# A two-layer hybrid block with 64 routed experts: the order of the expert weight loads, the expert slots, and three reorderings on the engines

## What is computed

```python
def moe_ffn(h, router_w, router_bias, w_gate, w_up, w_down, sh_gate, sh_up, sh_down):
    scores = jax.nn.sigmoid((h @ router_w).astype(jnp.float32))
    ...                                  # 4 of 8 groups, then the 8 best of their experts
    w = jnp.take_along_axis(scores, idx, axis=1)
    w = w / jnp.sum(w, axis=-1, keepdims=True) * ROUTED_SCALE
    shared = (jax.nn.silu(h @ sh_gate) * (h @ sh_up)) @ sh_down
    return routed_experts(h, idx, w, w_gate, w_up, w_down) + shared
...
    # of one expert e and its tokens xb
    hid = jax.nn.silu(xb @ w_gate[e]) * (xb @ w_up[e])      # 1024 -> 256
    return (hid @ w_down[e]) * wt[:, None]                  # 256 -> 1024
```

## Time and profile before

| | us |
|---|---|
| median of 3 runs | 2142.07 (2141.47 to 2149.24) |
| the profiled execution's own time | 2148.33 |
| its span, first to last instruction | 2146.50 |
| TensorE matmul busy | 1657.4 (77%) |
| VectorE, ScalarE, GpSimd busy | 905.9, 569.5, 347.5 |
| mean granted clock of TensorE | 0.91 |
| HBM read | 557.87 MB |

### The profile page before, as it was taken

One profiled execution on the slowest core, in us unless ns is written; L12 is line 12 of the kernel. 1 busy time (PEld: TensorE's weight loads), 2 busy tenths in 40 slices (PEclk: granted clock), 3 DMA queues, 4 the chain that ended last, 5 costly groups with the idle time before them and its releaser, 6 DMA issues. The chain is left out here.

```text
span 2146.5 us, 39607 instructions
## 1 busy us (share of the span) xinstructions
PE 1657.4 (77%) x11491; PEld 714.8 (33%) x11492; DVE 905.9 (42%) x3060; ACT 569.5 (27%) x1173; POOL 347.5 (16%) x357
## 2 busy tenths in 40 slices
PE   3999799858878888888886499698556656766675
PEld 2545554422223223322322455454212211212221
DVE  2245563364444444444446336543522322322334
ACT  2142352212322333333231214242111211221221
POOL 0001300002222222222220001210011111111110
PEclk8999799989999999999999699789888888988888
DMA  8315510447999899998837823813499989999974
GB/s 272 130 70 193 190 60 1 176 172 285 376 373 412 342 375 365 405 365 333 346 114 313 273 80 118 334 32 147 174 361 364 412 344 414 409 401 356 407 300 181
DMA packets 165603, 578.28 MB, mean 269 GB/s; under 512 B 24956, under 2 KB 29792, under 8 KB 148648
## 3 DMA queue, kind: packets, MB, share of 16 engines
q1 hardware_dynamic: 134592, 515.49, 61.9%
q0 software_dynamic: 24256, 60.03, 7.5%
q10 hardware_dynamic: 6696, 1.98, 0.4%
HBM read 557.87 MB, written 37.89 MB: 278 GB/s over the span
## 5 line engine op out<-in xcount | busy, mean ns | idle before, releaser
L1225 PE MATMUL bank<-arena 128*32 128x512 f32 x4160 | 544.1, 645 | 291.6 <-DMA arena<-in_exp_w_up 171.1
L1225 PEld LDWEIGHTS bank<-arena 128*32 128x32 f32 x4160 | 118.0, 115 | 494.8 <-issue 312.6
L692 POOL DMA_INDIRECT yrows<-arena x128 | 130.1, 1016 | 915.4 <-ACT arena L925 915.4
L1250 PE MATMUL bank<-arena 128*32 128x512 f32 x2048 | 247.0, 598 | 18.3 <-issue 16.5
L1735 DVE TENSOR_TENSOR arena<-arena,bank 64x512 f32<-64x512 f32 x130 | 88.4, 680 | 353.0 <-ACT arena L907 353.0
L920 ACT ACTIVATE arena<-bank 128x128 f32<-128x128 f32 x128 | 35.5, 278 | 685.6 <-PE bank L1281 685.6
L673 POOL DMA_INDIRECT arena<-hrows,arena x134 | 137.2, 1024 | 149.5 <-DVE arena L1709 108.5
L1693 DVE COPY arena<-arena 128x12 bf16 (+1 forms) x272 | 63.6, 234 | 193.4 <-issue 193.4
L991 PE MATMUL bank<-arena 128*128 128x512 f32 (+3 forms) x384 | 131.6, 504 | 11.7 <-DVE arena L1391 11.7
L1215 PEld LDWEIGHTS bank<-arena 128*128 128x128 f32 x528 | 73.8, 209 | 110.6 <-issue 110.6
L994 PE MATMUL bank<-arena 128*128 128x512 f32 (+1 forms) x256 | 100.0, 552 | 0.0
(11 more groups left out here) (304 smaller groups left out, 1910.2 us busy)
## 6 DMA issues: line engine op xcount, KB each, us to landing
arena<-in_exp_w_gate SPq DMA_DIRECT2D x128, 1024.0 KB
arena<-in_exp_w_up SPq DMA_DIRECT2D x128, 1024.0 KB
arena<-in_exp_w_down SPq DMA_DIRECT2D x128, 1024.0 KB
arena<-in_w_ada SPq DMA_DIRECT2D x10, 3072.0 KB
arena<-yrows SPq DMA_DIRECT2D x24, 1024.0 KB, 16.2
arena<-in_w_ada SPq DMA_DIRECT2D x8, 2048.0 KB
arena<-in_w_in SPq DMA_DIRECT2D x8, 2048.0 KB
arena<-in_w_out SPq DMA_DIRECT2D x4, 2048.0 KB
```

The lines of the kernel that those rows point to most:

```text
L692: pool.indirect_dma_start(out=yrows, out_offset=bass.IndirectOffsetOnAxis(ap=SIXS[u], axis=0), in_=YSB[u], in_offset=None, bounds_check=2 ...
L1225: ins = pe.matmul(bank[0][r:r + UNIT, :], XGT[:, c, un, hh, :], wv[un][:, :, hh, c, :], start=(c == 0), stop=(c == 3))
L1250: ins = pe.matmul(bank[2][r:r + UNIT, :], HIDT[:, c, UNIT * un:UNIT * un + UNIT], wv[un][:, c, cg * 512:(cg + 1) * 512], start=(c == 0), s ...
```

## The change

- **Order of the loads.** Refilling goes by expert n: first gate and up of expert n+4 (after the last gate-and-up product of expert n), then down of expert n+3 (after the last down product of expert n-1). So on the queue gate and up stand one expert ahead of down. Down of expert 3 is no longer loaded ahead of the loop, and down of the last expert is issued behind it. `TABP` gets a leading zero, so that expert n-1's entry exists for n = 0, and is read twice for each expert.
- **Semaphores.** Gate and up count on `sp_up`, not on `sp_land`, and SP no longer waits for a slot's last loads to have landed before it refills it.
- **Slots.** `exp_slot` gives expert 2's slot the place over `rH`, and expert 3's the third ring place; the first four experts are then loaded in the order 0, 1, 2, 3 (before: 0, 1, 3, 2), behind the same four events.
- **TensorE.** `meta` ("picking") moves from the head of an iteration to behind the down product of the one before; the table word is loaded once for each block, one block ahead, behind the transposes of the tokens, and carried in two registers; `b // 2` and `b % 2` are worked out behind the gate-and-up product.
- **ScalarE.** `silu` is cut in two, and the copy of the tokens (`xe`) stands between `lower_rows` and `silu`.

```diff
@@ -113,7 +113,8 @@
-        ring = [rRING + 6144 * k for k in range(3)] + [rH]
+        ring = [rRING + 6144 * k for k in range(3)]
+        exp_slot = [ring[0], ring[1], rH, ring[2]]
@@ -233,7 +234,7 @@
-        TABP = arena[0:1, o:o + NE].bitcast(I32); o += NE
+        TABP = arena[0:1, o:o + NE + 1].bitcast(I32); o += NE + 1
@@ -269,7 +270,8 @@
-        sp_land = [sem(f"sp_land{k}") for k in range(NSLOT)]
+        sp_land = [sem(f"sp_land{k}") for k in range(3)]
+        sp_up = [sem(f"sp_up{k}") for k in range(NSLOT)]
@@ -526,45 +526,50 @@
                 def load_up(e, k):
-                    w = at(ring[k], 2, 2, 4, HID)
+                    w = at(exp_slot[k], 2, 2, 4, HID)
                     for j, src in enumerate((eg, eu)):
...
                                      src[bass.ds(l * NE + e, 1)].rearrange("a (h p c) n -> p (a h) (c n)", h=2, c=4)
-                                     ).then_inc(sp_land[k], 16)
+                                     ).then_inc(sp_up[k], 16)
                 def load_down(e, k):
-                    sp.dma_start(at(ring[k] + 4096, 2 * DM),
+                    sp.dma_start(at(exp_slot[k] + 4096, 2 * DM),
                                  ed[bass.ds(l * NE + e, 1)].rearrange("a (p c) n -> p (a c n)", c=2)).then_inc(sp_dn[k], 16)
+                def blocks_up_to(j):
+                    return sp.snap((sp.value_load(TABP[0:1, bass.ds(j, 1)], min_val=0, max_val=MAXU) + 1) // 2)
+
...
-                    units_up_to = sp.value_load(TABP[0:1, bass.ds(i * NSLOT + u, 1)], min_val=0, max_val=MAXU)
-                    used = sp.snap((units_up_to + 1) // 2)
-                    sp.wait_ge(sp_land[u], i * 32 + (base_land[u] + 32))
-                    sp.wait_ge(sp_dn[u], i * 16 + 16)
-                    sp.sem_inc(sp_go, 1)
-                    sp.wait_ge(pe_gu, used + 1)
+                    k = (u + NSLOT - 1) % NSLOT
+                    sp.wait_ge(pe_gu, blocks_up_to(i * NSLOT + u + 1) + 1)
                     sp.sem_inc(sp_go, 1)
                     load_up(i * NSLOT + (NSLOT + u), u)
-                    sp.wait_ge(pe_dn, used + 1)
+                    sp.wait_ge(pe_dn, blocks_up_to(i * NSLOT + u) + 1)
                     sp.sem_inc(sp_go, 1)
-                    load_down(i * NSLOT + (NSLOT + u), u)
-
-
-                for e in (0, 1, 3, 2):
-                    if e < 3:
+                    load_down(i * NSLOT + (NSLOT + u - 1), k)
+
+
+                for e in range(NSLOT):
+                    if e < 2:
                         sp.wait_ge(*done_of[P_OUT + e])
-                    else:
+                    elif e == 2:
                         sp.wait_ge(pe_sh, 4)
                         sp.wait_ge(pool_hr, 16 * NTS)
+                    else:
+                        sp.wait_ge(*done_of[P_SH])
                     load_up(e, e)
-                    load_down(e, e)
+                    if e < NSLOT - 1:
+                        load_down(e, e)
                 sp.wait_ge(v_tab, 1)
...
                         reload(i, u)
+                sp.wait_ge(pe_dn, blocks_up_to(NE - NSLOT) + 1)
+                sp.sem_inc(sp_go, 1)
+                load_down(NE - 1, NSLOT - 1)
                 for k in range(NSLOT):
-                    sp.wait_ge(sp_land[k], base_land[k] + 32 * (NE // NSLOT))
+                    sp.wait_ge(sp_up[k], 32 * (NE // NSLOT))
                     sp.wait_ge(sp_dn[k], 16 * (NE // NSLOT))
@@ -900,26 +905,30 @@
-                def silu(val, free):
+                def lower_rows(val, free):
                     act.wait_ge(pe_gu, val + 1)
...
+
+                def silu(val):
                     act.wait_ge(v_gu, val)
...
                 xe(1)
-                silu(1, None)
+                lower_rows(1, None)
                 xe(2)
+                silu(1)
                 act.preload_act_table(ACT.Silu)
...
                         act.activation(HIDT, bank[5][:, 0:2 * SLOTS].rearrange("p (c s) -> p c s", c=2), ACT.Copy).then_inc(a_h, 1)
-                        silu(i * 2 + (u + 2), i * 2 + (u + 1))
+                        lower_rows(i * 2 + (u + 2), i * 2 + (u + 1))
                         xe(i * 2 + (u + 3))
+                        silu(i * 2 + (u + 2))
                         act.wait_ge(pe_dn, i * 2 + (u + 2))
@@ -1217,7 +1226,7 @@
-                    wv = [at(ring[k], 2, 2, 4, HID) for k in ks]
+                    wv = [at(exp_slot[k], 2, 2, 4, HID) for k in ks]
@@ -1230,9 +1239,9 @@
-                    pe.wait_ge(sp_land[k], e * 8 + (base_land[k] + 32 - 8 * k))
+                    pe.wait_ge(sp_up[k], e * 8 + (32 - 8 * k))
...
-                        pe.wait_ge(sp_land[k2], e * 8 + (base_land[k2] + 40 - 8 * k2))
+                        pe.wait_ge(sp_up[k2], e * 8 + (40 - 8 * k2))
@@ -1242,7 +1251,7 @@
-                    wv = [at(ring[k] + 4096, 2, DM) for k in ks]
+                    wv = [at(exp_slot[k] + 4096, 2, DM) for k in ks]
@@ -1251,9 +1260,12 @@
-                def experts_of(b):
...
-                    both = pe.value_load(TABK[0:1, bass.ds(b, 1)], min_val=0, max_val=2 * NE - 2)
+                def experts_word(b):
...
+                    return pe.value_load(TABK[0:1, bass.ds(b, 1)], min_val=0, max_val=2 * NE - 2)
...
+                def experts_of(both):
@@ -1287,7 +1299,11 @@
-                _, _, step = experts_of(0)
+                word = experts_word(0)
+                word_now = pe.alloc_register(f"word_now{l}")
+                word_next = pe.alloc_register(f"word_next{l}")
+                pe.reg_mov(word_now, word)
+                _, _, step = experts_of(word)
@@ -1299,12 +1315,12 @@
+                meta(4, 3)
+                pe.reg_mov(word_next, experts_word(1))
...
-                    meta(b + 4, b + 3)
-                    e, slot, step = experts_of(b + 1)
-                    half = pe.snap(b // 2)
-                    odd = pe.snap(b % 2)
+                    word = pe.snap(word_next)
+                    e, slot, step = experts_of(word)
@@ -1317,11 +1333,15 @@
                     in_slots(slot, step, up_and_turn)
+                    half = pe.snap(b // 2)
+                    odd = pe.snap(b % 2)
                     with pe.If(odd == 0):
...
                         turn_tokens(1, half * 16 + 32)
-                    now, slot_now, step_now = experts_of(b)
+                    now, slot_now, step_now = experts_of(pe.snap(word_now))
+                    pe.reg_mov(word_now, word)
+                    pe.reg_mov(word_next, experts_word(b + 2))
                     pe.wait_ge(a_h, b + 1)
@@ -1330,6 +1350,7 @@
+                    meta(b + 5, b + 4)
@@ -1610,7 +1631,8 @@
-                dve.wait_ge(v_pcl, 5)
+                dve.memset(TABP[0:1, 0:1], 0).then_inc(v_pcl, 1)
+                dve.wait_ge(v_pcl, 6)
@@ -1672,7 +1694,7 @@
-                link(dve.tensor_copy(TABP, PEND[0:1, :]))
+                link(dve.tensor_copy(TABP[0:1, 1:NE + 1], PEND[0:1, :]))
```

More of the change, by code:

```diff
@@ L426, in landed @@
             return sp_land[k], 16 * sum(d for m, d in enumerate(dmas_of[:n + 1]) if slot_of(m) == k)
-        base_land = [16 * sum(d for m, d in enumerate(dmas_of) if slot_of(m) == k) for k in range(NSLOT)]
         with nc.Block() as block:
```

## The result

The changed kernel took **2071.20 us** (median of four executions, 2068.59 to 2071.68), the kernel before beside it 2143.94 (2141.47 to 2149.24, four): a ratio of 0.9655, 95% interval 0.9634 to 0.9677. The profiled execution took 2068.59 us with a span of 2066.8, against 2148.33 and 2146.5: 79.7 us less. Later the same file ran twice more, in other sets of runs on two chips, and took 2095.63 and 2097.32 us, with the kernel before unchanged at 2147.

A forecast was written before the change was run, and what follows sets the result against it. TensorE, held by its sequencer, was taken to bound layer 0, and a loop of waits around loads layer 1. 42 + 32 + 2 = 76 us off gave 2066 us from the median, range 2036 to 2106.

The forecast's parts named there:

- rival 2: Layer 0: another wait takes the gap ahead of the gate-and-up product, layer 0 keeps 8 us; 2100 us, chance 0.13.
- Layer 1, forecast 32: Layer 1's loop: the new load order keeps the queue full and fills the holes, 32 us less, bounds 15 and 41.
- The loop of waits: Layer 1: SP's queue stands behind the down product, this behind the next gate-and-up product, that behind loads; no engine full.
- rival 1: Loads can't be packed closer, 414 GB/s not holding for 500 us; 2127 us, chance 0.05.
- Rival 3: Layer 1: the loop of waits stays, SP still behind a down product; layer 1 gives 10, 2088 us, chance 0.12.
- Layer 0, forecast 42: Layer 0's loop, paced by TensorE: 0.75 us less a block, capped by loads, 42 us less, bounds 25 and 58.
- rival 4: Gathers starve TensorE: a fuller queue makes GpSimd's gather later than its reader needs; slower, 2174 us, chance 0.04.
- the loads' limit of 49: Layer 0: what loads allow, 45 us of fillable DMA time plus 2.5 and 2; smaller than TensorE's 58.
- the gap shrinks to nothing: Layer 0, TensorE's wait ahead of the gate-and-up product, mean 0.86 us: it closes, taken as 0.75 us a block.
- the cover of SiLU and the product behind it: ScalarE's SiLU and product L1737 come up to 0.6 us later, covered by 24 matmuls (2.78 us) before the hidden transposes.
- It is what makes this gain possible: ScalarE's token copy ahead of SiLU comes 0.4 us or more earlier, so the wait for it doesn't hold the product.
- the 45 on the loads' side: Layer 0, 500 to 1075 us: DMA share 0.94 against 1.02 when full, so 45 us can be filled.

The follow-up runs named there:

- no_gather: The changed kernel with the loop's gathers replaced by a plain copy of 16 rows (products come out wrong): 78.7 us less than after_third.
- pe_act: The kernel before with the change's TensorE and ScalarE programs, loads as before: 13.9 us less than the kernel before.
- after_third: The changed kernel unedited, run a third time as the yardstick of its set: 2097.32 us.

## Why the prediction was right, and where it was not

**Time.** 2071.20 against 2066, inside the range; on the later chips 2095.63 and 2097.32, inside it too, but 30 us from the forecast and near the 2100 of rival 2. That the first number came so close is in part luck: it needed counts on time, which the prediction didn't consider and which only the first set had.

**Layer 1, forecast 32, measured 31.8.** This step held everywhere: 28 us with the loads alone, 31 in every set with the whole change, whatever TensorE did. The loop of waits was what made the holes; the share reached 0.99 (0.98 was the mark), and a stretch of 100 us at 413 GB/s answers rival 1. *no_gather* points the same way, though it has two blocks fewer besides. Rival 3 fell by its number, 31.8 and not 10; its mechanism is still seen in seven of the chain's 16 up loads. The limit of 358 GB/s in the Trainium skill ("DMA: Bandwidth & Descriptors", Specifications) doesn't hold in these runs: 393 to 396 GB/s over 500 us.

**Layer 0, forecast 42, measured 45.1 in the first set and 20 in the later ones.** The median period came to 7.23 us (7.25 forecast) from 8.04, with the wait ahead of the product at 5.6 us in 17 of 56 blocks. From the fifth block on the mean is 7.51, since nine of them take over 8.5 us. One of them shows rival 4's mechanism, once in 56 blocks (the wait for L1224 above):

```profile
910.10 0.75 PE L1224 MATMUL bank<-arena 128*128 128x128 f32 x4 [0.82 <-DMA arena<-hrows,arena]
```

```profile
912.60 3.11 PE L1259 MATMUL bank<-arena 128*32 128x512 f32 x16 [1.75 <-issue]
```

A gather comes 0.82 us late, the down product then starts 1.75 us late and takes 3.11 us where 1.92 is usual, and the block takes 10.83 us. The granted clock was 0.60 from 912.6 to 915.7 us and 1.00 before.

That the gain came so near the loads' limit of 49 doesn't test this limit: no run has the old order of the loads with counts on time.

The step that failed on the later chips is the one that follows "the gap shrinks to nothing": I took 0.75 us a block off and named the cover of SiLU and the product behind it, but not that of the hidden copy, which the down product waits for. With the late count it has none: the gap ahead of L1234 closes and 33 to 37 us open ahead of L1259 (*pe_act*, and in *after_third*, 652 to 1069 us):

```profile
PE bank L1259 <- issue: 36.7, 49, 1.8
```

That is rival 2's case, another wait takes the gap, at another place than I looked for it. I could have seen it. The prediction says that only one wait of TensorE matters in the stretch of the earlier trace rows, but the same view has a second one, ahead of the down product:

```profile
PE bank L1250 <- issue: 9.5, 14, 1.1
```

And a count that is late shows in the kernel before as well (0.29 us in the mean of layer 0, over 0.1 in 49 of 80 blocks), mostly hidden there: the later end of the copy still came in time for the down product.

**"It is what makes this gain possible"**, of ScalarE's copy, is half right. Without it the gain isn't lost: taking it out costs 11 us, taking TensorE's part out 14.5. And each of them alone leaves 35 to 41 us of the wait ahead of the gate-and-up product from 660 to 1060 us.

**Loads' part of layer 0.** With the loads alone layer 0 gives 8 us, as TensorE sets its pace; the 45 on the loads' side were room, which only a faster TensorE fills.

## What to carry to other kernels

When a gap ahead of one operation closes, look at the next wait of the same engine and at what it waits for, one by one: the gain goes to the second longest chain, and its slack is in the trace of before. Parts of a change are to be compared within one set of runs on one chip with the whole change beside them; a whole from elsewhere made an interaction of 25 us out of nothing. Where a queue issues in order, put the load whose place comes free first ahead of one that waits for a later product.

## What the runs showed of the hardware that I had not expected

- In the changed kernel the semaphore count of a finished transpose came 0.87 to 0.88 us late (means of layer 0) on two chips, when GpSimd ran the instruction of an indirect gather at the same time (1.02 us each). Counts of the gate-and-up products came 0.07 us behind their ends and those of the down products 0.04 (medians of layer 0; at most 0.30 and 0.05). The late count came about half a microsecond behind the end of the gather's instruction. It came on time without the gather, and with the transposes 1.6 us sooner. In the first set it came on time with both side by side, in 128 of 128 blocks. What differed there stays open: no run tells a property of the chip from one of that session, and by which way the gather holds the count back wasn't tried either.
- An unchanged file differs by 1.2% between sets of runs (2071.20 against 2095.63), with 0.2% within each, while the medians of the kernel before lie within 0.15%: a median and its interval say nothing of that.
